# Expert weights reloaded half by half, an early buffer for expert 2's up weights, and more identity products

## The chip, the cores and the metric

The kernel runs on one core of a Trainium2 chip. The metric is the device time of one execution in microseconds (us). The kernel before took 1606.25 us, the median of three runs (1605.87 to 1609.35).

## What is computed

Two transformer blocks over 512 tokens of 1,024 features. The first has attention and a gated feed-forward part; the second has a state-space mixer, windowed attention and, last, a hierarchical mixture of experts. Only the end of the second block matters here:

```python
x = x + g1 * (jnp.concatenate([ssd_x, attn_x], axis=-1) @ w_out[layer])
h2 = rms_norm_2(x, norm2[layer]) * (1 + sc2) + sh2
moe_x = hier_moe(h2.reshape(b * n_tok, d), w_group[layer], b_group[layer], w_expert[layer],
                 b_expert[layer], w_gate[layer], w_up[layer], w_down[layer])
x = x + g2 * moe_x.reshape(b, n_tok, d)
...
return rms_norm_2(x, norm_final)
```

`hier_moe` picks for each token one of four groups and in it two of eight experts. There are 32 experts. Each has a gate and an up matrix of 1,024 x 512 and a down matrix of 512 x 1,024, all float32: 2.1 MB each (the trace writes 2048 KB), 6.3 MB an expert, 201 MB in all. Every matrix is used once.

## The kernel before

**Stages.** First block, second block's mixers, then `norm2_2`, then routing, then the expert stage. Routing computes the logits, the two best experts of each token, each token's place in its expert's block of 64 places, and a table from places to tokens. In the expert stage every expert works on one block of 64 places.

**Engines in routing.** PE makes the logits (ticks `halves` and `logits`), the ranks (`rank`), the table (`table`) and the rows of keys (`rows`). DVE computes what lies between in small steps (L2217 to L2309). Between `places` and `table` it computes the later blocks (L2298 to L2303), which PE doesn't wait for. While PE waits it multiplies the identity by itself (`unread`), with a result that nobody reads; each such product shows as two records.

**Expert n on the engines.** POOL gathers the 64 tokens of expert n from the stored normalised tokens in HBM by an indirect DMA (`gather`, L938), two experts ahead. PE transposes them (`tokens_in_place`, 8 transposes), DVE scales and shifts them (L2316, L2319), and PE multiplies them with gate and up (`gate_and_up`). That is one loop of KT = 8 steps over j; at j = 0 and j = 4 it waits for the first and the second half of both matrices, and the 32 records are two halves of the array's columns for gate and for up. ACT copies the result, PE transposes it (`hidden_transposed`), ACT and DVE form the hidden values (L2327), and PE multiplies with down (`down`, 16 records). PE also adds the results of a pair of experts to the tokens, two of four token tiles per expert (`pair_piece`, 32 records an odd expert has ahead of its gate products, 32 an even one has ahead of its down products, in two groups of 16). So the order on PE in a pair is: pieces, gate and up of the odd expert, transposes, a wait for DVE (L2327), its down; gate and up of the even expert, transposes, pieces, its down.

**Slots.** There are two sets of three slots of 2.1 MB: set 0 in the arena for even experts, set 1 in the ring for odd ones (`EXPERT_SLOTS`). One extra buffer, `early_gate`, lies over the normalised tokens once they have been stored to HBM (`h_stored`). It holds expert 2's gate, and no other weights.

**The order of the loads.** All weights are loaded by one queue, SP's, in this written order: expert 0 (six transfers, the halves of gate and up are 1 MB each and down is 2 MB); expert 1, once the output projection's last bank is filled; the store of the normalised tokens; expert 2's gate, in two halves, into `early_gate`, when the store has landed; expert 2's up and down into set 0; expert 3; the final gain; then a loop over experts 4 to 31. In `load_expert` (L757 to L779) SP waits for `gu_filled`, the count of experts whose gate and up products are done, and then issues all halves of gate and up; then it waits for `y_filled`, the count of finished down products, and issues down. Semaphores `first_in` and `second_in` count landed halves, `down_in` landed down matrices.

**Small state.** `sm` (`ssd_small`, 128 x 960 floats) is used by the state-space mixer and by the rows of the modulation, and no more from routing on. POOL's indirect and distance loads are written by a descriptor store in SBUF, of the size that the program asks for.

Of the kernel before, what the change touches and what calls it, by code (L numbers as in the profile page):

```python
# [14 lines left out]
P = 128  # L15
# [9 lines left out]
E = 32  # L25
# [133 lines left out]
def two_blocks(nc, consts_d, rope1_d, dist_d, h_d, inp, out):  # L159
    ctx = ExitStack()  # L160
    with ctx:
# [3 lines left out]
        def sb(name, shape, dt=F32):  # L165
            return ctx.enter_context(nc.sbuf_tensor(name, shape, dt))
# [28 lines left out]
        gains = sb("gains", [P, 6, KT])  # L195
        convw = sb("convw", [P, 224])
        ada_bias = sb("ada_bias", [P, 6, KT])
# [3 lines left out]
        mod_gain = sb("mod_gain", [P, 3, KT])  # L201
        gates = sb("gates", [P, 2, D])
        dt_bias, a_log = sb("dt_bias", [P, 16]), sb("a_log", [P, 16])
        d_skip, sinks, route_bias = sb("d_skip", [P, 8]), sb("sinks", [P, 8]), sb("route_bias", [P, 36])
# [6 lines left out]
        arena_at = nc.sbuf_base  # L211
        arena = sb("arena", [P, ARENA])


# [35 lines left out]
        def packed(size_of, start=0, of=arena, limit=ARENA):  # L250
# [6 lines left out]
            return views  # L257

        hT_flat = hT[:, :, :].rearrange("p j n -> p (j n)")
        ring_flat = ring[:, :, :].rearrange("p a n -> p (a n)")  # L260
# [33 lines left out]
        skip_x = carve(2048 + 2 * (T + CTX), 512, of=slot)  # L294
        sm = sb("ssd_small", [P, 10, 96])
        cat = xn
# [384 lines left out]
        index_ready, late_ready = sem("index_ready"), sem("later_block_ready")  # L681
        xt_filled, xt_scaled, xt_ready = sem("expert_x_filled"), sem("expert_x_scaled"), sem("expert_x_ready")
        gu_filled, gu_ready = sem("gate_up_filled"), sem("gate_up_ready")
        ht_filled, silu_ready, hid_ready = sem("hiddenT_filled"), sem("expert_silu"), sem("expert_hidden")
# [82 lines left out]

        def load_expert(sp, e, par, reuse, early=False):

            if reuse is not None:  # L770
                sp.wait_ge(gu_filled, reuse)
            for half in range(2):
                for i in range(2):
                    if i or not early:
                        load_rows(sp, e, par, i, half)
            if reuse is not None:
                sp.wait_ge(y_filled, reuse)
            sp.dma_start(EXPERT_SLOTS[3 * par + 2], inp["w_down_2"].rearrange("a e (p f) d -> (a e) p (f d)", f=4)[e]).then_inc(
                down_in[par], 16)  # L779

        def modulation(sp, parts):
# [22 lines left out]
        def _(sp):  # L804
# [34 lines left out]

            banks.filled(sp, ("out2", TT - 1, 1))  # L840
            load_expert(sp, 1, 1, None)
            normed.wait(sp, ("norm2_2", TT - 1, 0))
            sp.dma_start(h_d.rearrange("(t p) n -> p t n", p=P), xn[:, 0:TT, :]).then_inc(h_stored, 16)
# [3 lines left out]
            for half, landed in enumerate((first_in, second_in)):  # L847
                sp.wait_ge(landed[0], 16)
                load_rows(sp, 2, 0, 0, half, early_gate)
            load_expert(sp, 2, 0, 1, True)  # L850
            load_expert(sp, 3, 1, 2)
            sp.wait_ge(gu_filled, 3)
            sp.dma_start(final_gain, inp["norm_final_2"].partition_broadcast(P)).then_inc(final_in, 16)
            with sp.Fori(2, E // 2) as it:
                for par in range(2):
                    load_expert(sp, 2 * it + par, par, 2 * it + par - 1)
# [450 lines left out]
        def _(pe):  # L1307
# [379 lines left out]
            route_pe.tick(mm(ps[2][:, TT * E:2 * TT * E], C("one").broadcast_to([P, P]), hot, True, True), "rank")  # L1687
            unread(ps[3], 34)
            route.wait(pe, "places")
# [20 lines left out]

            def gate_and_up(n, par, kpar, gate=None):

                gate_w, up_w = EXPERT_SLOTS[3 * par] if gate is None else gate, EXPERT_SLOTS[3 * par + 1]
                pe.wait_ge(xt_ready, n + 1)
                for j in range(KT):
                    if j % 4 == 0:
                        for i in range(2):
                            pe.wait_ge((first_in, second_in)[j // 4][2 * par + i], 16 * kpar + 16)  # L1720
                    for half, w in enumerate((gate_w, up_w)):
                        last = mm(ps[1][half * BLK:(half + 1) * BLK, :], xT[:, par, j, :], w[:, j * EF:(j + 1) * EF],
                                  j == 0, j == KT - 1)
                last.then_inc(gu_filled, 1)

# [41 lines left out]

            unread(ps[0], 6)
            tokens_in_place(0, 0, 0)
            route_act.wait(pe, "rows")  # L1770
            for n in range(E):
                if n % 2 == 1:
                    for pair, t in pieces_of_turn(n):
                        pair_piece(pair, t)
                gate_and_up(n, n % 2, n // 2, early_gate if n == 2 else None)
                if n + 1 < E:
                    tokens_in_place(n + 1, (n + 1) % 2, (n + 1) // 2)
                hidden_transposed(n, n % 2)
                if n % 2 == 0:
                    for pair, t in pieces_of_turn(n):  # L1780
                        pair_piece(pair, t)
                down(n, n % 2, n // 2, n if n else None)
# [633 lines left out]
```

## Time and profile before

| | before |
|---|---|
| time, median of 3 runs | 1606.25 us |
| time of the profiled execution | 1606.26 us |
| span of the profiled execution | 1604.4 us |
| PE busy | 1499.6 us, 93% of the span |
| DVE busy | 913.7 us, 57% |
| ACT busy | 518.9 us, 32% |
| mean of the DMA engines' rate | 192 GB/s |
| mean granted TensorE clock | 0.98 of full |

The table is an average over stages with different limits. The page's slices are 40.1 us each, so slices 27 and 28 are routing and the start of the experts (1,043 to 1,123 us). A DMA row gives the time from issue to landing. A wait is put down to what ended it.

### The profile page before, as it was taken

Reading aid. Unit: us, or ns where it says so; the run is one execution under the profiler, and the core shown is the slowest. Engines: PE = TensorE matmul, PEld = TensorE weight load, DVE = VectorE, ACT = ScalarE, POOL = GpSimd, SP = SyncE. Lnnn points to the kernel's source line nnn. Section 1 sums busy time; section 2 is a strip of 40 time slices with the busy share of each in tenths; the row PEclk is TensorE's granted clock in tenths of the full one; section 3 lists DMA queues with packets and bytes.
Section 4 is the critical chain, followed back from the end, with each engine's and each line's share of the span. In section 5 each row is a group of like instructions: output and inputs, shape, how many; then the busy total and the mean of one; then the engine's idle time right before and its main releaser. Section 6 shows DMA issues by size and latency. Waiting matters only on the chain.

```text
span 1604.4 us, 21206 instructions
## 1 busy us (share of the span) xinstructions
PE 1499.6 (93%) x8171; PEld 1041.4 (65%) x8171; DVE 913.7 (57%) x1697; ACT 518.9 (32%) x938; POOL 99.3 (6%) x132
## 2 busy tenths in 40 slices
PE   7999998999999999999999897988999999999896
PEld 6776667888888878878887686873444444344343
DVE  4745774467787567753764677472444454344435
ACT  5445665333343332243426534221101101010112
POOL 0000000000000000000004132001101101000100
PEclk9999998999999999999999999999999999999998
DMA  8212011255544357613020000565999999999993
GB/s 254 78 54 73 2 50 50 70 173 140 155 130 120 110 171 271 212 39 119 27 69 11 1 1 3 208 262 206 414 399 405 410 401 411 399 405 402 410 411 160
DMA packets 112365, 308.39 MB, mean 192 GB/s; under 512 B 13983, under 2 KB 65535, under 8 KB 90763
## 3 DMA queue, kind: packets, MB, share of 16 engines
q1 hardware_dynamic: 108755, 299.08, 50.4%
q0 software_dynamic: 3200, 7.87, 1.6%
q8 instruction: 66, 1.08, 0.3%
q14 instruction: 32, 0.26, 0.0%
q10 hardware_dynamic: 312, 0.10, 0.0%
HBM read 306.99 MB, written 4.22 MB: 194 GB/s over the span
## 4 chain that ended last, share of the span: by engine, by line
PE 73%; DMA 9%; DVE 8%; ACT 4%; issue 3%; SPq 2%; POOL 0%; DVEq 0%; ACTq 0%; POOLq 0%
PE bank L1309 68%; DMA arena<-in_w_up 8%; PE bank L1312 5%; SPq L826 1%; DVE arena L2192 1%; DVE ring L2134 0%; DVE hTc L2316 0%; ACT weights_high L971 0%; SPq L766 0%; DMA ring<-in_w_in 0%; DVE x_res L2205 0%; DVE ring L2136 0%; DVE xn L2204 0%; DVE arena L2386 0%; ACT hT_high L1031 0%
## 5 line engine op out<-in xcount | busy, mean ns | idle before, releaser
L1309 PE MATMUL bank<-weights_high,hT_high 128*128 128x512 f32 (+2 forms) x736 | 255.1, 385 | 12.6 <-ACT arena L1058 5.3
L1807 DVE TENSOR_TENSOR weights_low<-ring,weights_high 128x2048 fp32r<-128x2048 f32 (+2 forms) x61 | 135.6, 2224 | 139.8 <-ACT weights_high L971 138.9
L1309 PE MATMUL bank<-weights_low,hT_high 128*128 128x512 f32 (+2 forms) x560 | 212.6, 380 | 0.0
L971 ACT ACTIVATE weights_high<-ring 128x2048 fp32r<-128x2048 f32 (+2 forms) x61 | 113.4, 1859 | 190.7 <-PE bank L1309 158.0
L1309 PEld LDWEIGHTS bank<-weights_high,hT_high 128*128 128x128 f32 x736 | 139.0, 189 | 40.3 <-issue 8.4
L1309 PE MATMUL bank<-hT_high,weights_high 128*128 128x512 f32 x416 | 163.8, 394 | 0.8 <-DVE hT_low L1845 0.8
L1309 PE MATMUL bank<-hT_high,weights_low 128*128 128x512 f32 x416 | 161.9, 389 | 0.0
L1309 PE MATMUL bank<-hT_low,weights_high 128*128 128x512 f32 x416 | 161.9, 389 | 0.0
L2316 DVE TENSOR_TENSOR hTc<-bank,mod_gain 128x512 f32<-128x512 f32 x32 | 22.1, 691 | 193.9 <-PE bank L1312 193.9
L1309 PE MATMUL bank<-arena,hTc 128*64 128x512 f32 x496 | 115.6, 601 | 7.3 <-DMA arena<-in_w_up 5.7
L1309 PE MATMUL bank<-ring,hTc 128*64 128x512 f32 (+1 forms) x544 | 121.4, 583 | 0.6 <-DMA ring<-in_w_up 0.6
L1309 PEld LDWEIGHTS bank<-weights_low,hT_high 128*128 128x128 f32 x560 | 106.1, 189 | 19.5 <-issue 0.2
L1309 PEld LDWEIGHTS bank<-hT_high,weights_high 128*128 128x128 f32 x416 | 78.1, 188 | 20.2 <-issue 3.4
L1276 ACT ACTIVATE hTc<-bank 128x512 f32<-128x512 f32 x32 | 19.1, 597 | 221.9 <-PE bank L1309 221.9
L1309 PE MATMUL bank<-ring,hT 128*64 128x512 f32 x256 | 71.8, 713 | 18.3 <-DVE hT L2327 18.3
L1309 PEld LDWEIGHTS bank<-hT_high,weights_low 128*128 128x128 f32 x416 | 78.1, 188 | 16.3
L1309 PEld LDWEIGHTS bank<-hT_low,weights_high 128*128 128x128 f32 x416 | 78.1, 188 | 16.0
L1309 PEld LDWEIGHTS bank<-ring,hTc 128*64 128x64 f32 (+1 forms) x544 | 41.6, 140 | 71.9 <-issue 70.8
L1309 PEld LDWEIGHTS bank<-arena,hTc 128*64 128x64 f32 x496 | 38.1, 138 | 76.9 <-issue 76.9
L1309 PE MATMUL bank<-weights_high,hT_low 128*128 128x512 f32 (+1 forms) x224 | 84.0, 375 | 0.0
L1288 ACT ACTIVATE expert_y_high<-arena 128x512 fp32r<-128x512 f32 x32 | 20.2, 631 | 192.9 <-DVE arena L2350 192.9
L1135 ACT ACTIVATE arena<-bank,convw 128x512 f32<-128x512 f32 x44 | 34.3, 778 | 145.8 <-PE bank L1309 145.8
(329 smaller groups left out, 2483.7 us busy)
## 6 DMA issues: line engine op xcount, KB each, us to landing
arena<-in_w_up SPq DMA_DIRECT2D x32, 1024.0 KB, 20.0
arena<-in_w_down SPq DMA_DIRECT2D x16, 2048.0 KB, 22.3
ring<-in_w_gate SPq DMA_DIRECT2D x32, 1024.0 KB, 17.6
ring<-in_w_up SPq DMA_DIRECT2D x32, 1024.0 KB, 19.6
ring<-in_w_down SPq DMA_DIRECT2D x16, 2048.0 KB, 21.9
arena<-in_w_gate SPq DMA_DIRECT2D x30, 1024.0 KB, 18.6
xn<-in_w_ada SPq DMA_DIRECT2D x48, 512.0 KB, 4.7
ring<-in_w_up SPq DMA_DIRECT2D x44, 512.0 KB, 5.2
```

What stands on the lines that cost most here:

```text
L826: sp.dma_start(dst, src).then_inc(more_in, 16)
L971: high_ready.tick(s.activation(part_view(w_high, key), raw_view(key), ACT.Copy), k)
L1135: tap_mid.tick(s.activation((conv_g, conv_v)[gv][:, f % 2, :], bank[:, :], ACT.Identity, scale=convw[:, 44 + ch:45 + ch], bias=convw[:, 13 ...
L1276: s.activation(gu[:, par, :], ps[1][:, :], ACT.Copy).then_inc(gu_ready, 1)
L1288: s.activation(y_high[:, place, :], y_scaled, ACT.Copy).then_inc(y_high_ready, 1)
L1309: return nc.tensor.matmul(o, lhsT, rhs, start=start, stop=stop)
L1312: return nc.tensor.transpose(o, i, ident[0:n, 0:n])
L1807: low_ready.tick(v.tensor_tensor(part_view(w_low, key), raw_view(key), part_view(w_high, key), ALU.subtract), k)
L2192: ins = v.tensor_scalar(decay[:, i % 3, g * 4 + h, :], bank[:, h * P:(h + 1) * P], sm[:, 7, a:a + 1], 0.0, ALU.subtract, ALU.min)
L2316: v.tensor_tensor(xT[:, par, :, :], ps[0][:, :].rearrange("p (j n) -> p j n", j=KT), wide(mod_gain[:, 2, :], BLK), ALU.mult).then_inc(xt_s ...
```

## The change

- A buffer `early_up` of one slot's size is added, and `sm` is laid over it. Expert 2's up weights are loaded into it in two halves, right behind expert 1's loads; expert 2's gate and up products read both early buffers. `convw` lies elsewhere, and the descriptor store shrinks (the new argument `dynamic_dma_scratch_size=4096`; the default is 16384).
- `load_expert` is split into `load_gate_and_up` and `load_down`. The first halves of a reload now wait for a new semaphore, `gu_half_done`, which PE increments after step j = 3 of the products, and the second halves for `gu_filled`.
- The order on SP's queue becomes: expert 2's gate; a wait for both matrices of expert 2; expert 4's gate and up; expert 2's down; expert 3; the final gain; expert 4's down; expert 5; then the loop from expert 6.
- The identity products go from 34 to 44 ahead of the table products, from 6 to 13 ahead of the first tokens' transposes, and 7 new ones lie between these and expert 0's products.

```diff
-        convw = sb("convw", [P, 224])
...
+        convw = sb("convw", [P, 224])
...
+        early_up = sb("early_up", [P, UNIT])
...
+        sm = carve(0, 10, 96, of=early_up)
...
-        sm = sb("ssd_small", [P, 10, 96])
...
+        gu_half_done = sem("gate_up_first_rows_done")
...
-        def load_expert(sp, e, par, reuse, early=False):
-
-            if reuse is not None:
-                sp.wait_ge(gu_filled, reuse)
-            for half in range(2):
-                for i in range(2):
-                    if i or not early:
-                        load_rows(sp, e, par, i, half)
+        def load_down(sp, e, par, reuse):
+
             if reuse is not None:
                 sp.wait_ge(y_filled, reuse)
...
+        def load_gate_and_up(sp, e, par, reuse):
+
+            for half, used in enumerate((gu_half_done, gu_filled)):
+                if reuse is not None:
+                    sp.wait_ge(used, reuse)
+                for i in range(2):
+                    load_rows(sp, e, par, i, half)
+
+        def load_expert(sp, e, par, reuse):
+
+            load_gate_and_up(sp, e, par, reuse)
+            load_down(sp, e, par, reuse)
...
             load_expert(sp, 1, 1, None)
+            for half, landed in enumerate((first_in, second_in)):
+                sp.wait_ge(landed[1], 16)
+                load_rows(sp, 2, 0, 1, half, early_up[:, :])
             normed.wait(sp, ("norm2_2", TT - 1, 0))
...
                 load_rows(sp, 2, 0, 0, half, early_gate)
-            load_expert(sp, 2, 0, 1, True)
+            for landed in first_in[0:2] + second_in[0:2]:
+                sp.wait_ge(landed, 32)
+            load_gate_and_up(sp, 4, 0, 1)
+            load_down(sp, 2, 0, 1)
             load_expert(sp, 3, 1, 2)
             sp.wait_ge(gu_filled, 3)
             sp.dma_start(final_gain, inp["norm_final_2"].partition_broadcast(P)).then_inc(final_in, 16)
-            with sp.Fori(2, E // 2) as it:
+            load_down(sp, 4, 0, 3)
+            load_expert(sp, 5, 1, 4)
+            with sp.Fori(3, E // 2) as it:
                 for par in range(2):
                     load_expert(sp, 2 * it + par, par, 2 * it + par - 1)
...
-            unread(ps[3], 34)
+            unread(ps[3], 44)
...
-                gate_w, up_w = EXPERT_SLOTS[3 * par] if gate is None else gate, EXPERT_SLOTS[3 * par + 1]
+                gate_w, up_w = EXPERT_SLOTS[3 * par:3 * par + 2] if early is None else early
...
+                    if j == 3:
+                        last.then_inc(gu_half_done, 1)
                 last.then_inc(gu_filled, 1)
...
-            unread(ps[0], 6)
+            unread(ps[0], 13)
             tokens_in_place(0, 0, 0)
+            unread(ps[1], 7)
             route_act.wait(pe, "rows")
...
-                gate_and_up(n, n % 2, n // 2, early_gate if n == 2 else None)
+                gate_and_up(n, n % 2, n // 2, (early_gate, early_up[:, :]) if n == 2 else None)
...
-    nc = bacc.Bacc("TRN2", target_bir_lowering=False, num_devices=1)
+    nc = bacc.Bacc("TRN2", target_bir_lowering=False, num_devices=1, dynamic_dma_scratch_size=4096)
```

## Rows read from the trace of the kernel before

**Rows 1.** The page's slices of 40 us: what the DMA engines moved.

```profile
GB/s 254 78 54 73 2 50 50 70 173 140 155 130 120 110 171 271 212 39 119 27 69 11 1 1 3 208 262 206 414 399 405 410 401 411 399 405 402 410 411 160
```

**Rows 2.** A window: busy time by engine, granted clock, DMA share, GB/s.

```profile
1330.00:1560.00 230.00, 215.56 (x1099) 92.07 (x1098) 96.08 (x157) 23.20 (x43) 17.94 (x27) 0.97 1.01 406
```

**Rows 3.** PE's waits, 1090 to 1600 us: total, times, longest.

```profile
PE bank L1309 <- DVE hT L2327: 19.6, 17, 1.2
PE bank L1309 <- DMA arena<-in_w_up: 5.7, 5, 2.4
...
PE bank L1309 <- DMA ring<-in_w_up: 0.6, 2, 0.3
```

**Rows 4.** The chain that ended last, expert stage: start, us, what.

```profile
1145.35 12.11 PE bank L1309 x48
...
1176.74 10.52 PE bank L1309 x48
...
1329.16 12.24 PE bank L1309 x48
...
1342.98 24.98 DMA arena<-in_w_up
...
1534.04 25.28 DMA arena<-in_w_up
```

**Rows 5.** SP's queue in order of time: start, time of the issue.

```profile
1053.42 0.38 SPq L843 DMA_DIRECT2D normed_tokens<-xn  x1
1071.21 0.80 SPq L766 DMA_DIRECT2D xn<-in_w_gate  x2
1099.24 0.80 SPq L766 DMA_DIRECT2D arena<-in_w_up  x2
...
1126.80 0.36 SPq L766 DMA_DIRECT2D arena<-in_w_gate  x1
```

**Rows 6.** The chain, first gather: start, us, what.

```profile
1083.98 3.69 DMA xn<-normed_tokens,token_index
```

**Rows 7.** DMA issues of two windows: KB each, median us to landing.

```profile
xn<-in_w_gate SPq DMA_DIRECT2D x2, 1024.0 KB, 6.5
...
arena<-in_w_up SPq DMA_DIRECT2D x2, 1024.0 KB, 22.2
xn<-normed_tokens,token_index POOLq DMA_INDIRECT x1, 8.9
```

**Rows 8.** Windows around expert 0, columns as in rows 2.

```profile
1080.00:1084.00 4.00, 4.00 (x23) 4.00 (x23) 1.39 (x6) 0.00 (x0) 0.20 (x2) 0.57 0.00 0
...
1092.00:1096.00 4.00, 4.00 (x16) 1.56 (x14) 0.00 (x0) 0.00 (x0) 0.00 (x0) 0.75 0.06 18
...
1096.00:1100.00 4.00, 4.00 (x24) 1.89 (x20) 0.00 (x0) 0.60 (x1) 0.00 (x0) 1.00 0.00 0
1100.00:1116.00 16.00, 13.61 (x69) 5.73 (x69) 6.50 (x12) 1.99 (x4) 2.86 (x4) 1.00 0.86 313
1100.00:1148.00 48.00, 44.45 (x227) 18.86 (x227) 20.65 (x34) 5.21 (x10) 5.65 (x8) 0.97 0.96 378
```

**Rows 9.** PE in order of time: start, us, operation, [idle before].

```profile
1068.96 7.76 PE L1309 MATMUL bank<-const 128*128 128x128 f32 x68
1079.27 2.81 PE L1309 MATMUL bank<-arena 128*128 128x94 f32 x16 [2.55 <-DVE arena L2296]
...
1087.81 1.06 PE L1312 MATMUL bank<-const,xn 64*128 64x64 f32 x8 [1.73 <-DMA xn<-normed_tokens,token_index]
1090.43 8.78 PE L1309 MATMUL bank<-arena,hTc 128*64 128x512 f32 x32 [1.55 <-issue]
...
1105.63 7.04 PE L1309 MATMUL bank<-ring,hTc 128*64 128x512 f32 x32
```

**Rows 10.** DVE in order of time, end of routing.

```profile
1080.77 0.16 DVE L2303 CAST later_blocks<-later_counts 1x15 int32<-1x15 f32 x1
1082.19 0.21 DVE L2307 TENSOR_SCALAR arena<-bank 128x47 f32<-128x47 f32 x1 [1.26 <-PE bank L1309]
```

More of the change, by code:

```diff
@@ L1709, in tokens_in_place, with gate_and_up @@
                 last.then_inc(xt_filled, 1)
-            def gate_and_up(n, par, kpar, gate=None):
-                gate_w, up_w = EXPERT_SLOTS[3 * par] if gate is None else gate, EXPERT_SLOTS[3 * par + 1]
+            def gate_and_up(n, par, kpar, early=None):
+                gate_w, up_w = EXPERT_SLOTS[3 * par:3 * par + 2] if early is None else early
                 pe.wait_ge(xt_ready, n + 1)
```

## The prediction, made before the changed kernel was run

> **What bounds the kernel now.** I read the page's slices first. From the 29th slice on (1,123 us) the rate stands at 399 to 414 GB/s until the last slice but one; the three slices ahead of it, in which the first experts' weights come in and routing runs, have 206 to 262 [rows 1]: the expert stage streams weights as fast as they come, and there is room ahead of it. A window over the second half of that stage has the DMA engines at a share of 1.01 with 406 GB/s, while PE is busy 215.56 of 230 us [rows 2]. Both are nearly full, so the next view is PE's waits. From expert 0's first product to the end of the stage PE waits for weights 5.7 + 0.6 = 6.3 us, and 17 times for about 1.2 us on DVE's addition to the tokens (L2327), which the change leaves [rows 3]. The chain says where the 6.3 us lie: up to 1,329 us it holds only PE's own pace, and from 1,343 us on it goes through the landing of an up half [rows 4].
>
> Two rates follow. PE's pace: the products after the gap recur at 1145.35 and, six pairs of experts later, at 1329.16: 183.81 / 6 = 30.64 us a pair. The weights' pace: expert 18's second up half lands at 1342.98 + 24.98 = 1367.96, expert 30's at 1534.04 + 25.28 = 1559.32, six pairs too: 191.36 / 6 = 31.89 us a pair [rows 4]. So DMA is 1.25 us a pair slower than PE. It begins with a lead, uses it up at about expert 18, and then PE waits. What a change in the loads is worth is decided by the lead, and it is worth at most the 6.3 us that PE waits; anything more has to come from PE's own path.
>
> **Part 1, expert 2's up weights into a buffer of their own.** Two transfers of 1 MB each are issued right behind expert 1's, ahead of the store of the normalised tokens at 1053.42 [rows 5]. Their own waits on SP are for expert 0's halves, which were issued some 37 us earlier; they cost nothing. The queue is full there: SP's next issue, which waits for the store to land, comes 17.8 us after the store's, at 1071.21 [rows 5]; the landing is at about 1070.8. 2.1 MB at 406 GB/s [rows 2] are 5.2 us, so the store lands at about 1076.0, and SP's next two issues (expert 2's gate) move to about 1076.4. Behind SP's wait stand only the later weights. Behind the store stands also the first gather, issued at 1083.98 [rows 6]: 8 us of cover, 6.8 after the gain of part 3, so it costs nothing. The gate transfers take 6.5 us to landing [rows 7] and land at about 1083.6 instead of 1078.4; the first gather's own data follow its issue, then at 1082.8, by more than a microsecond. They just miss each other (rival 2).
>
> **Part 2, reloading by halves, and expert 4's gate and up ahead of expert 2's down.** Before, the queue is empty from about 1078 to 1100 (0 GB/s in 1096 to 1100) [rows 8], since the up slot is reloaded only at 1099.24, the slot of expert 0's gate lies unused until 1126.80, and from 1100 to 1116 the share is only 0.86 [rows 5, 8]. After, expert 4's first halves go out when four of expert 0's eight steps are done, its second halves after the other four. With expert 0 starting at 1089.2 and lasting 7.04 us (part 3) these are 1092.8 and 1096.3, 4.2 MB; expert 2's down (2.1 MB) goes out at about 1102.7, expert 3's halves at 1106.0 and 1109.5 (2.1 MB each): from 1094 to 1116 there is always something queued. Bytes by 1116: before, 16 us at 313 GB/s, 5.0 MB [rows 8]; after, 22 us x 0.406 = 8.9 MB, and 2.1 MB of part 1 lie in place: 6.0 MB or 15 us more. This lead isn't all kept. With expert 3's weights in, the slots are full, and PE sets when they come free; by about 1148 all that the slots allow is loaded, which I sum to 22.8 MB (18.9 of weights from expert 4's gate to expert 5's up, 0.5 of final gain, 1.3 of gathers, 2.1 early) against 48 us x 378 GB/s = 18.1 MB before [rows 8], a lead of 4.7 MB or 11.5 us; a restart of an empty queue takes about 1 us (issue at 1099.24, data from about 1100) [rows 5, 8]. Say 10 us. From there DMA falls back by 1.25 us a pair, as before, with no more empty stretches. PE comes to the same place 3.0 us earlier (part 3), so the weights are ahead of their old place by 10 - 3.0 = 7 us as PE sees them. The deficit was 6.3 us. So all waits for weights should go, with 0.7 us to spare at expert 30: **-6.3 us**, and the bound is then PE alone. What is late next is that pace of 30.64 us a pair, with the 1.2 us gap on L2327. The added semaphore increment on an instruction that is there anyway shows in no row; the nearest ones, the increments on each last product, leave no visible gap, so its cost is 0, at most some tenths over 32 experts. SP's new waits (gu_half_done) have only weights behind them; expert 5's loads stand behind the wait for expert 3's down, as before.
>
> **Part 3, more identity products.** In two windows of 4 us the granted clock is 0.57 at 1080 to 1084 and 0.75 at 1092 to 1096, where full is 1.00 [rows 8]: the lower of the two levels, 1.2 instead of 2.4 GHz, for part of each. What PE did before: it was idle 2.55 us ahead of 1079.27, and 1.73 and 1.55 us ahead of 1087.81 and 1090.43 [rows 9]. Ten more products are 20 records at 7.76 / 68 = 0.114 us, 2.3 us: the row ends at 1076.72 + 2.3 = 1079.0, just inside 1079.27. Seven more (1.6 us) go ahead of the first gather's arrival, seven new ones (1.6 us) between its transposes and expert 0's products (gap 1.55). All three fit their gaps by some tenths, and if each overran by that, it would cost 0.3 us in all.
> - The table products: 16 records of 94 columns take 2.81 us [rows 9]. At full clock an estimate from the 0.114 us for 128 columns is 16 x 0.084 + 0.15 = 1.5 us, 1.3 less. But DVE is busy with the later blocks until 1080.77 + 0.17 = 1080.94, and reads the table from 1082.19 now [rows 10]: it can't start before 1081.0, so the gain is 1.2 us, not 1.3. The token index, POOL's gather (3.69 us, [rows 6]) and expert 0 follow at the same distance: **-1.2 us**.
> - Expert 0's 32 products take 8.78 us, expert 1's 7.04 [rows 9]: **-1.7 us** if the clock holds.
> Bounds: 0 if the clock falls anyway, -3.0 if both hold; I take both, since the long gaps go and the one that is left, about 1.0 us ahead of the gather, is no longer than gaps of 1.2 us that at full clock PE mostly passes.
>
> **Part 4, addresses and the smaller descriptor store.** Moved small tiles cost nothing that a row shows. Fewer descriptors could make POOL's gathers wait for older ones; no row shows such a wait. A gather is issued one expert (15 us) ahead of its use and lands in 8.9 us in the full queue [rows 7]; bounds 0 and 0.5 us, I take 0.
>
> **The sum** against the profiled execution: span 1604.4, its time 1606.26 (1.9 around it), equal to the median of 1606.25. 1606.25 - 1.2 - 1.7 - 6.3 = **1597.0 us**. Bounds of the terms: 0 to 1.2, 0 to 1.7, and 3 to 6.3.
>
> **The rivals.**
> 1. *DMA stays the bound.* The lead is 0.7 us too large in my sum, and 10 us is made of a 11.5 and a guess of the losses. If halves give more empty moments while PE sets the pace, or the rate is 402 rather than 406 GB/s (1%, 4 us over the stage), 2 to 4 us of waiting remain at experts 26 to 30. For: shares of 1.01 all along [rows 2]. Against: the lead's size. Time 1599 to 1601.
> 2. *The start gains nothing.* The gate transfers and the first gather overlap. In an empty queue a gather takes 3.69 us of the chain [rows 6]; in the full one the issue-to-landing time is 8.9 us [rows 7], against about 4.7 counted the same way: up to 4 us more on the critical path, which cancels part 3. Then expert 0 starts late, the weights are further ahead, and only the 6.3 us go: 1600 to 1601. For: a margin of 1 us. Against: the gate's last bytes, not its landing, are what counts.
> The Trainium skill (DMA: Bandwidth & Descriptors, section Queues, rings and completion order) says that each DMA engine takes turns between the queues that have work, a packet at a time, so that a gather isn't held until the weights ahead of it are done. By that rule an overlap costs less than the rest of the gate transfers, and the start would keep part of its 3 us, which makes about 1598; the gathers of the full queue agree, since they land in 8.9 us where an up half issued beside them takes 22.2 [rows 7].
> 3. *The clock falls at every gap* (slower). Every second pair has a cold stretch: 48 products take 12.11 us at 1145.35 and 10.52 at 1176.74 [rows 4], 1.6 us. There are 17 gaps of 1.2 us [rows 3] and seven such cold stretches before the last expert. If an earlier start shifts things so that each gap is followed by one, ten more cost 16 us, and the 1.7 of expert 0 is lost too: 1606.25 - 9.2 + 17.7 = 1614.8. It decides from six more on; eight make it slower by over 0.2%. Against: a cold stretch delays the next gap, and the pattern of every second pair held over 250 us.
> The Trainium skill (TensorE: Matmul & The Clock Gate, section Part 1: The HAM clock gate) says that the watch on activity runs freely and isn't tied to the kernel. By it one cold stretch more or less is chance, 1.6 us either way, and no run of before here can show which.
> 4. *Fewer cold stretches*, or a lead that also hides a gap: 1592 to 1595.
>
> **Chances.** Forecast (1595 to 1599) 0.55; rival 1 0.16; rival 2 0.12; rival 3 0.05; rival 4 0.07; the change brings less than 3.2 us by several of these together 0.05. Two runs of one kernel differ here by about 0.2%, 3.2 us, and less than that can't be told from no change. Faster by more: 0.55 + 0.16 + 0.12 + 0.07 = 0.90, less 0.02 for the ends of rivals 1 and 2; same 0.07; slower 0.05. The range reaches over rivals 1 and 2 and part of 4: 1593.5 to 1601.5, leaving out about 0.17.
>
> **What would show it.** Right: no wait of PE for in_w_up, or under 1 us; DMA at over 300 GB/s from 1094 and below that once around 1126 to 1135 and again near 1148; expert 0's products at 1089.2 in 7.04 us; clock 1.00 from 1076 to 1096; pairs still at 30.6 us. Wrong: waits for weights from expert 24 on (rival 1), a first gather over 4.5 us (rival 2), 12.1 us for the 48 products in each pair (rival 3), the store landing after 1081.

## The result

The changed kernel takes 1597.87 us, the median of 13 runs (1594.51 to 1604.32), beside 1606.66 us of the kernel before in 13 runs (1604.28 to 1610.44). The ratio is 0.9947, with a 95% interval of 0.9937 to 0.9956: 8.5 us faster, 7.1 to 10.1. The forecast was 1597.0 us and 9.2 us faster.

The page of the changed kernel: the span, PE's busy time, and the rate in slices of 39.8 us.

```profile
span 1593.5 us, 21287 instructions
...
PE 1497.4 (94%) x8219; PEld 1043.0 (65%) x8219; DVE 914.3 (57%) x1697; ACT 519.2 (33%) x938; POOL 99.4 (6%) x132
...
GB/s 255 71 62 74 1 48 54 53 178 152 133 145 115 98 180 269 240 27 133 27 54 27 1 1 1 211 263 274 354 404 412 409 409 407 399 407 393 410 412 178
```

The profiled execution took 1595.31 us, in the faster half of the 13 runs. Against [rows 1] the 28th slice rises from 206 to 274 GB/s, since bytes come earlier, and the 29th falls from 414 to 354, since there is a dry moment in it. The rate afterwards is the same.

PE's waits from 1085 to 1600 us: total, times, longest. They answer to [rows 3].

```profile
PE bank L1326 <- DVE hT L2347: 19.6, 17, 1.2
PE bank L1326 <- DMA arena<-in_w_up: 1.9, 2, 1.4
PE bank L1329 <- DMA xn<-normed_tokens,token_index: 1.0, 1, 1.0
```

The 5.7 + 0.6 us of waiting for weights have become 1.9 us; the 17 gaps on DVE stand as they were. They are on the step that forms the hidden values (L2327 before, L2347 after), which the prediction called the addition to the tokens.

The chain that ended last in the changed kernel: start, us, what. It answers to [rows 4] and [rows 6].

```profile
1083.57 3.63 DMA xn<-normed_tokens,token_index
...
1143.32 10.52 PE bank L1326 x48
...
1327.18 10.52 PE bank L1326 x48
...
1492.49 27.06 DMA arena<-in_w_up
...
1523.93 26.15 DMA arena<-in_w_up
```

Six pairs take 1327.18 - 1143.32 = 183.86 us, 30.64 a pair, as before. A landing enters the chain only from 1492 us on, where before it did from 1343 on.

PE around the start of the experts: start, us, operation, and in brackets the idle time before. It answers to [rows 9].

```profile
1069.32 9.99 PE L1326 MATMUL bank<-const 128*128 128x128 f32 x88
1079.64 2.02 PE L1326 MATMUL bank<-arena 128*128 128x94 f32 x16 [0.33 <-DVE arena L2316]
1081.50 1.98 PE L1326 MATMUL bank<-const,arena 128*128 128x128 f32 x16
...
1087.34 1.06 PE L1329 MATMUL bank<-const,xn 64*128 64x64 f32 x8 [0.96 <-DMA xn<-normed_tokens,token_index]
1088.33 1.83 PE L1326 MATMUL bank<-const 128*128 128x128 f32 x14
1090.09 7.09 PE L1326 MATMUL bank<-arena,hTc 128*64 128x512 f32 x32
```

The gaps of 2.55, 1.73 and 1.55 us are 0.33, 0.96 and none. The table products take 2.02 us instead of 2.81 and expert 0's products 7.09 instead of 8.78.

Windows of the changed kernel, columns as in rows 2; they answer to [rows 8].

```profile
1100.00:1148.00 48.00, 45.56 (x234) 19.02 (x236) 19.76 (x33) 5.04 (x10) 4.74 (x7) 1.00 0.93 366
1148.00:1330.00 182.00, 175.03 (x906) 75.59 (x904) 80.20 (x131) 19.15 (x36) 16.71 (x24) 0.97 1.01 408
1128.00:1132.00 4.00, 4.00 (x22) 1.47 (x20) 3.11 (x6) 0.00 (x0) 0.00 (x0) 1.00 0.13 44
...
1080.00:1084.00 4.00, 4.00 (x38) 4.00 (x38) 1.72 (x8) 0.48 (x1) 0.61 (x2) 1.00 0.97 408
```

The clock at 1080 to 1084 is full where it was 0.57. The queue now runs dry once, at 1128 to 1132, where all slots are full and PE sets the pace. Its issues in order of time show the new order; they answer to [rows 5].

```profile
1053.76 0.38 SPq L855 DMA_DIRECT2D normed_tokens<-xn  x1
1077.29 0.81 SPq L768 DMA_DIRECT2D xn<-in_w_gate  x2
1093.86 0.33 SPq L768 DMA_DIRECT2D arena<-in_w_gate  x1
...
1097.22 0.33 SPq L768 DMA_DIRECT2D arena<-in_w_gate  x1
```

**Where the time went.** The issue of expert 1's first load lies at 1046.98 us before and at 1047.32 after, so I count from there to the end of the span: 557.4 us before, 546.2 after, 11.2 less. On PE's side:

- To expert 0's first product: 43.45 and 42.77 us, 0.7 less. Expert 0's products: 1.7 less.
- Waits for weights: 4.4 less. Each such wait costs about 0.17 us beyond the idle time shown: 16 products without a wait take 3.44 us from start to start, those ahead of a wait take that, the idle time and 0.17. Five waits fewer are 0.8 us.
- Cold stretches (the granted clock is at the lower level, and a set of 16 products takes 1.65 us longer): the trace's clock record has eight between 1100 us and the last products before (from 1145, 1207, 1268, 1329, 1391, 1456, 1521 and 1582 on) and six after (from 1203, 1265, 1295, 1357, 1418 and 1480 on), 3.3 less.

These are 10.9 of the 11.2 us. The queue's side gives a shorter account. In both executions PE still waits for expert 30's second up half. Its products start again, when that half has landed, 512.5 us after expert 1's first load before and 502.9 after: 9.6 us earlier. What follows takes 1.7 us less, since before it held the cold stretch of 1582 and after it holds none. So in both the landing of these weights sets the end, and what PE gained on its way there, at the start and by one cold stretch fewer, counts only as far as the queue came earlier too.

The gain of this pair of executions is larger than the 8.5 us of all runs; two cold stretches less may be no more than chance.

### The profile page after: what moved, and what is told of

Its sections match the earlier page's. It is cut to its first block, busy times and chain, and to the rows that moved or that the text cites. A ratio compares the mean times of both kernels' runs of the same rounds, so it can differ in the third digit from the quotient of the medians.

```text
span 1593.5 us, 21287 instructions
## 1 busy us (share of the span) xinstructions
PE 1497.4 (94%) x8219; PEld 1043.0 (65%) x8219; DVE 914.3 (57%) x1697; ACT 519.2 (33%) x938; POOL 99.4 (6%) x132
## 4 chain that ended last, share of the span: by engine, by line
PE 78%; DVE 9%; ACT 4%; DMA 4%; issue 3%; SPq 1%; POOL 0%; DVEq 0%; ACTq 0%; POOLq 0%
PE bank L1326 72%; PE bank L1329 6%; DMA arena<-in_w_up 3%; SPq L835 1%; DVE arena L2212 1%; DVE hTc L2336 1%; DVE ring L2154 0%; ACT weights_high L988 0%; DMA ring<-in_w_in 0%; DVE hT L2347 0%; DVE x_res L2225 0%; DVE ring L2156 0%; DVE xn L2224 0%; DVE arena L2406 0%; ACT hT_high L1048 0%
## 5 line engine op out<-in xcount | busy, mean ns | idle before, releaser
L1326 PE MATMUL bank<-arena,hTc 128*64 128x512 f32 x480 | 106.1, 593 | 1.9 <-DMA arena<-in_w_up 1.9
L1326 PE MATMUL bank<-ring,hT 128*64 128x512 f32 x256 | 68.6, 685 | 18.4 <-DVE hT L2347 18.4
L2356 DVE TENSOR_TENSOR x_res<-bank,x_res 128x512 f32<-128x512 f32 x128 | 79.4, 683 | 2.3 <-PE bank L1326 1.3
```

The lines of the kernel that those rows point to most:

```text
L1326: return nc.tensor.matmul(o, lhsT, rhs, start=start, stop=stop)
L2356: last = v.tensor_tensor(side, ps[4 + 2 * (t % 2) + half][:, :], side, ALU.add)
```

## The experiments

Each kernel ran in turn with the kernel before on the same chip. "Stage" is the time from expert 1's first load to the end of the span, as above, in the profiled execution. "Last landing" is the time from the same load to where expert 30's products go on after their wait for the second up half; it tells how far ahead the queue is. Us, from the traces:

| kernel | last landing | stage | cold stretches after expert 0's first products |
|---|---|---|---|
| before | 512.5 | 557.4 | 8 |
| changed | 502.9 | 546.2 | 6 |
| 1, identity products only | 510.1 | 553.4 | 5 |
| 1, all but these | 509.4 | 552.7 | 8 |
| 2, halves only | 510.4 | 553.6 | 6 |
| 2, changed without halves | no wait there | 552.6 | 9 |
| 4, gaps filled | 502.6 | 546.0 | 0 |
| 5, gate beside the gather | 510.4 | 553.7 | 6 |

**1. The parts apart.** First only the identity products, in the kernel before:

```diff
-            unread(ps[3], 34)
+            unread(ps[3], 44)
...
-            unread(ps[0], 6)
+            unread(ps[0], 13)
             tokens_in_place(0, 0, 0)
+            unread(ps[1], 7)
```

> The kernel before with only the added identity products (44, 13 and 7). Theory (the start and the weights are separate terms): expert 0 starts 0.7 us earlier and its products take 7.0 us instead of 8.8. In the kernel before the reloads hang on PE's progress, so the queue starts 2.4 us earlier too, and the whole stage moves: 1606.7 - 2.4 = 1604.3 us. Rival (the weights are the bound and the start is hidden behind them): no change, 1606.7, with PE waiting 8.7 us for in_w_up instead of 6.3.

Measured: ratio 0.9984 (0.9970 to 0.9999), 2.6 us faster. PE's waits in this kernel:

```profile
PE bank L1309 <- DMA arena<-in_w_up: 9.0, 7, 2.2
...
PE bank L1309 <- DMA ring<-in_w_up: 0.6, 1, 0.6
```

The theory holds: the last landing comes 2.4 us earlier (512.5 to 510.1), just what PE's start gives, since the reloads hang on PE and come earlier too. The waits rise all the same, from 6.3 to 9.6 us: this execution has two cold stretches fewer ahead of expert 30 than that of the kernel before (five against seven), and the 3.3 us that PE gained there it spent waiting for weights.

Then everything but the identity products:

```diff
-            unread(ps[3], 44)
+            unread(ps[3], 34)
...
-            unread(ps[0], 13)
+            unread(ps[0], 6)
             tokens_in_place(0, 0, 0)
-            unread(ps[1], 7)
```

> The changed kernel with the identity products of before (34, 6 and none). Theory: the waits of PE for in_w_up fall from 6.3 us to under 1.9, since PE comes 2.4 us later and the weights don't; expert 0's products take 8.8 us. 1597.9 + 2.4 - 1.5 = about 1599 us, at most 1600.3. Rival (the identity products carry the gain): 1604 or more.

Measured: ratio 0.9958 (0.9944 to 0.9972), 6.7 us faster. PE's waits:

```profile
PE bank L1329 <- DMA xn<-normed_tokens,token_index: 2.2, 1, 2.2
...
PE bank L1326 <- DMA arena<-in_w_up: 1.2, 1, 1.2
```

The waits fall to 1.2 us and the time to about where it was expected. Over all runs the loads carry most of the gain, the start 2 to 3 us: 2.6 + 6.7 = 9.3 us beside 8.5 for both together. In this trace they don't add up so simply. The last landing is 3.1 us earlier than before, where the two parts together give 9.6: expert 0's products take 10.02 us here and its down products are cold too, and as long as SP waits for PE to free the slots, each such loss delays the loads behind it.

**2. The halves.** Only the halves, in the kernel before:

```diff
-            if reuse is not None:
-                sp.wait_ge(gu_filled, reuse)
-            for half in range(2):
+            for half, used in enumerate((gu_half_done, gu_filled)):
+                if reuse is not None:
+                    sp.wait_ge(used, reuse)
                 for i in range(2):
```

> The kernel before with nothing but the first halves of gate and up reloaded once step 3 is done. Theory (the lead in bytes ahead of the PE-bound stretch decides): only the up half of expert 2 goes out 4 us earlier, 1 MB, and expert 3's first halves; the empty moments before 1116 us shrink. The lead grows by 2 to 4 us, PE's waits fall to 2 to 4 us: 1603 to 1605 us. Rival (finer reloading raises the rate while DMA is the bound): the rate over 1330 to 1560 us rises above 406 GB/s and the waits vanish: 1600.

Measured: ratio 0.9982 (0.9971 to 0.9993), 2.9 us faster, which is within what was expected. The profiled execution has 6.5 us of waits for weights, no fewer than the 6.3 before, but it has one cold stretch fewer ahead of expert 30 (six against seven), 1.7 us by which PE came earlier. The lead did grow: the last landing comes 2.1 us earlier (512.5 to 510.4), at the low end of the 2 to 4 expected, and the first wait for weights comes at expert 22 instead of 18. The rate over 1330 to 1550 us is 405 GB/s, so finer reloading doesn't raise the rate, and that rival falls.

Then the changed kernel without them:

```diff
-            for half, used in enumerate((gu_half_done, gu_filled)):
+            for half, used in enumerate((gu_filled, gu_filled)):
```

> The changed kernel with both halves waiting for the whole of the products, all else kept. Theory (lead): the first 2.1 MB of expert 4 go out 3.5 us later, at 1097.2 instead of 1093.9, and the queue has an empty moment at each expert while PE sets the pace, so the lead is 3 to 4 us smaller and PE's waits rise from 1.9 to 5 or 6 us: 1601 us. Rival (early buffer alone carries the lead): 1598, no difference from the changed kernel.

Measured: ratio 0.9969 (0.9957 to 0.9981), 5.0 us faster than before, 3.5 us of the changed kernel's gain lost; the two intervals just miss each other. The first 100 us from expert 1's first load, in the kernel before, the changed one and this one, and PE's waits in this one:

```profile
1046.98:1146.98 100.00, 85.30 (x508) 51.32 (x508) 49.68 (x143) 16.14 (x34) 11.20 (x15) 0.96 0.74 287
```

```profile
1047.32:1147.32 100.00, 89.85 (x572) 55.12 (x572) 50.02 (x144) 16.15 (x34) 11.21 (x15) 1.00 0.83 323
```

```profile
1046.94:1146.94 100.00, 89.59 (x558) 54.82 (x559) 49.72 (x143) 16.16 (x34) 11.23 (x15) 0.97 0.77 301
```

```profile
PE bank L1326 <- DMA arena<-in_w_up: 2.9, 2, 2.4
```

301 instead of 323 GB/s over 100 us are 2.2 MB or 5.4 us of lead lost, more than the 3 to 4 expected; of the 3.6 MB that the changed kernel is ahead of the kernel before, 1.4 are left. Part of it isn't the halves' own: expert 0's down products are cold in this execution (from 1101 us on), so PE frees the slots 1.7 us later; by that estimate some 3.7 us are the halves'. The waits rise by 1.0 us only, because PE too is slower here, by three cold stretches more than in the changed kernel. So the halves are worth 2.9 us of time in the kernel before and 3.5 in the changed one. This execution ends without a wait at expert 30, by PE's pace, so how their lead becomes these 3.5 us it doesn't show.

**3. The lead, measured by itself.** With most of the token pieces' products left out PE is soon ahead of the weights, and the queue's own schedule sets the end. The same edit went into the kernel before and into the changed one:

```diff
-                for k, place in enumerate(places):
-                    for part, y in enumerate((y_high, y_low)):
+                for k, place in enumerate(places[-1:]):
+                    for part, y in enumerate((y_high,)):
```

> The kernel before with two of the eight products of each token piece, so that PE does 3 us less in each pair of experts (three quarters of the sums are left out). PE is then faster than the weights from the start, and the end of the stage shows where the queue's own schedule ends. Theory: weights bound throughout, pairs at 31.9 us; PE, which waited 6.3 us at the end, waits far more, and the time stays near 1604 to 1606 us, less the last 1 us of pieces.

> The same products left out in the changed kernel. Theory (lead of 10 us): the changed queue's own schedule ends 9 to 11 us ahead of that of the kernel before, so the two light kernels differ by that, and this one ends at about 1595 us, no more than 2 us ahead of the changed kernel itself, whose margin was nearly used up. Rival (the changed kernel is PE-bound with room to spare): it ends 5 us or more ahead of the changed kernel, at 1592 or less.

Measured: ratios 0.9973 (0.9961 to 0.9984) and 0.9916 (0.9901 to 0.9931), medians 1602.23 and 1594.00 us; the first a little under the 1603 to 1605 expected. The two differ by 0.0057, 9.2 us; their stages, 552.4 and 543.3 us, by 9.1. PE waits for weights 21 and 20 times, from 1194 and from 1248 us on; first the light kernel before, then the light changed one:

```profile
PE bank L1309 <- DMA arena<-in_w_up: 21.9, 12, 3.0
PE bank L1309 <- DMA ring<-in_w_up: 13.5, 9, 2.7
```

```profile
PE bank L1326 <- DMA ring<-in_w_up: 13.9, 10, 2.6
PE bank L1326 <- DMA arena<-in_w_up: 13.5, 10, 2.6
```

So the lead is 9.2 us (forecast: 10). How near the changed kernel comes to its queue's own end is less sure. By the profiled executions the light changed kernel's stage is 2.9 us shorter, of which about 0.9 are pieces left out behind the last expert (from DVE's last step on expert 31's result to the start of DVE's last step on the output it takes 9.75 us instead of 10.64), so 2 us are left. By the ratios of all runs (0.9916 against 0.9947) it is 5.0 us faster, 4 without these pieces: more than the 2 expected and near the rival's 5. The profiled execution of the changed kernel is one of its faster ones; in the slower ones PE may have more of its own to lose, which no trace here shows.

**4. The clock's gaps filled.** In the changed kernel, five identity products in each gap of 1.2 us:

```diff
-                pe.wait_ge(hid_ready, n + 1)
-                pe.wait_ge(down_in[par], 16 * kpar + 16)
                 if read is not None:
                     pe.wait_ge(y_weighted, read)
+                if isinstance(n, int) and (n % 2 == 1 or n == 0):
+                    unread(ps[3], 5)
+                pe.wait_ge(hid_ready, n + 1)
+                pe.wait_ge(down_in[par], 16 * kpar + 16)
```

> The changed kernel with five identity products in each of the 1.2 us gaps ahead of an odd expert's down products (and expert 0's), into the bank that these products overwrite. Theory (weights and PE end together): the cold stretches between 1100 and 1550 us, six in the changed kernel, become fewer or vanish, PE's pair goes to 29.8 us, and PE then waits for weights instead: waits rise from 1.9 to about 10 us, and the time falls by 1 us at most, 1597 to 1598. Rival (PE alone is the bound): 1588 to 1590, 1.6 us for each cold stretch that goes. Second rival: the fill overruns the gap in each pair and costs 0.1 to 0.3 us each, 2 to 4 us slower.

Measured: 1595.76 us, ratio 0.9927 (0.9914 to 0.9941). Between 1100 us and the last products no cold stretch is left. A set of 48 products in the chain, as each pair has it, and PE's waits:

```profile
1330.14 10.54 PE bank L1326 x48
```

```profile
PE bank L1326 <- DMA arena<-in_w_up: 10.0, 7, 2.4
...
PE bank L1326 <- DMA ring<-in_w_up: 0.4, 1, 0.4
```

The pair goes to 29.8 us, and the waits rise from 1.9 to 10.4 us: in these two executions what the clock gives, the queue takes. The last landing is 502.6 us, the changed kernel's 502.9, and the stage 546.0 against 546.2. Over all runs it is faster than the changed kernel by 2.1 us by the medians and 3.2 by the ratios, more than the 1 us expected; the intervals overlap, so whether it beats it isn't settled.

The same with the queue out of the way. From expert 6 on only half of each down matrix is loaded (the products use stale rows for the other half), without and with filled gaps:

```diff
+            n = UNIT if isinstance(e, int) else HALF
+            sp.dma_start(EXPERT_SLOTS[3 * par + 2][:, 0:n],
+                         inp["w_down_2"].rearrange("a e (p f) d -> (a e) p (f d)", f=4)[e][:, 0:n]).then_inc(
```

> The changed kernel with only half of each down matrix loaded from expert 6 on (the products use stale rows for the other half), a sixth less bytes, so the queue can't be the bound. Theory (the changed kernel is PE-bound but for 1.9 us): PE's waits for weights are 0, pairs at 30.65 us, and the time is 1.5 to 2.5 us under the changed kernel, 1595.5 to 1596.5. Rival (the weights' traffic itself slows PE, ACT or DVE): pairs under 30.3 us and 1590 or less.

> The same with the 1.2 us gaps filled as in e7. Theory (in the changed kernel PE's clock and the queue each hide the other's gain): no cold stretch, no wait, pairs at 29.8 us, 10 us under e9: 1585 to 1587. Rival (filling a gap costs what the clock gives): within 3 us of e9.

Measured: 1597.1 us, ratio 0.9938 (0.9922 to 0.9954), and 1584.11 us, ratio 0.9854 (0.9837 to 0.9870). Neither waits for weights. The chain of the first, then of the second:

```profile
1144.43 12.19 PE bank L1328 x48
...
1328.34 12.22 PE bank L1328 x48
```

```profile
1145.71 10.52 PE bank L1328 x48
...
1324.55 10.52 PE bank L1328 x48
```

183.91 us for six pairs against 178.84: 30.65 and 29.81 us a pair. A sixth less bytes alone give 1.4 us by the ratio, and nothing that can be told from the changed kernel; the pairs keep their 30.65 us, so traffic doesn't slow PE. Filling the gaps on top of that gives 13.5 us more (0.0084, and 13.5 by the stages). It is the cold stretches: the first has nine from 1100 us on, 14.9 us at 1.65 each, and the second none, but one earlier, in the fill ahead of expert 0's products (14 records in 3.10 us instead of 1.83), 1.6 us with what it adds to these products. So PE and queue end together in the changed kernel: fewer bytes alone give 1.4 us, filled gaps alone 2 to 3, both together 15.

**5. The rival of the first gather.** Expert 2's gate load is held back until the table products are done:

```diff
             route_pe.wait(sp, "halves")
+            route_pe.wait(sp, "table")
             sp.wait_ge(h_stored, 16)
```

> The changed kernel with expert 2's gate load held back until the table products are done, so that its 2.1 MB run beside the first gather. Theory (price of the overlap that the prediction named as a rival): the first gather takes 2 to 4 us longer than 3.6, expert 0 starts that much later, and expert 4's halves follow. The later start is partly made good by fewer waits: 1599.5 to 1601.5 us. Rival, by the rule of the Trainium skill that the engines take turns between queues (DMA: Bandwidth & Descriptors, section Queues, rings and completion order): under 1.5 us longer, 1598 to 1599.5.

Measured: 1603.48 us, ratio 0.9976 (0.9965 to 0.9987), 4.7 us of the gain lost by the ratio. The gather in the chain, and two microseconds in which PE is idle while the DMA engines are full:

```profile
1084.19 7.97 DMA xn<-normed_tokens,token_index
```

```profile
1088.00:1090.00 2.00, 0.00 (x0) 0.00 (x0) 0.00 (x0) 0.00 (x0) 0.00 (x0) 1.00 1.05 324
```

The packets of SP's queue (q1, the weights) and POOL's (q0, the gathers), first in 1085 to 1088.3 us, then in 1088 to 1091: count, MB, share.

```profile
q1 hardware_dynamic: 188, 1.41, 101.4%
```

```profile
q0 software_dynamic: 140, 0.36, 53.1%
q1 hardware_dynamic: 63, 0.39, 37.9%
```

The gather takes 7.97 instead of 3.63 us, 4.3 more, not far from the 5.2 us of the 2.1 MB it ran beside. It was issued at 1084.19 us; up to 1088.3 only weights move, then both share the engines. PE, idle for 5.29 us, then has a cold stretch, and expert 0's products take 7.84 us. Expert 0's products end 6.6 us later than in the changed kernel, and the last landing comes 7.5 later: the start's delay goes into the queue in full. Both of my sizes for the whole were too small: 1599.5 to 1601.5 and less were expected.

**6. The small descriptor store alone,** in the kernel before:

```diff
-    nc = bacc.Bacc("TRN2", target_bir_lowering=False, num_devices=1)
+    nc = bacc.Bacc("TRN2", target_bir_lowering=False, num_devices=1, dynamic_dma_scratch_size=4096)
```

> The kernel before with nothing but the descriptor store at 4096 bytes. Theory: no gather or distance load waits for a descriptor, 1606.7, within 1 us of the kernel before; gathers still land 8 to 9 us after issue. Rival: gathers land later, and PE waits for tokens: 1608 or more.

Measured: ratio 1.0001 (0.9988 to 1.0014). Gathers land 8.3 us after their issue, against 8.1 in a like stretch of the kernel before; both stages are 557.4 us, both last landings 512.5. No cost shows.

**7. More lead.** Experiment 4 with both early buffers used a second time, for expert 5, and expert 7's gate and up loaded into the ring one turn earlier:

```diff
+            for half, used in enumerate((gu_half_done, gu_filled)):
+                sp.wait_ge(used, 3)
+                for i, into in enumerate((early_gate, early_up[:, :])):
+                    load_rows(sp, 5, 1, i, half, into)
             load_down(sp, 4, 0, 3)
...
+            load_gate_and_up(sp, 7, 1, 4)
+            load_down(sp, 5, 1, 4)
+            load_expert(sp, 6, 0, 5)
...
-                gate_and_up(n, n % 2, n // 2, (early_gate, early_up[:, :]) if n == 2 else None)
+                gate_and_up(n, n % 2, n // 2, (early_gate, early_up[:, :]) if n in (2, 5) else None)
```

> e7 with both early buffers used once more, for expert 5's gate and up, issued at about 1121 to 1124 us instead of 1137 to 1140, and expert 7's then in the ring at 1137 to 1140 instead of 1167 to 1170. Theory (the lead in bytes decides, and it grows by what the queue stood empty): the empty stretch at 1128 to 1132 goes, the lead grows by 2 to 4 us, PE's waits for weights fall from 10.4 to 6 to 8 us, and the time from 1595.8 to 1592 to 1594. Rival (order in the queue matters more: expert 7's early bytes delay expert 6's): no gain or a loss, 1596 to 1598.

Measured: 1595.08 us, ratio 0.9926 (0.9911 to 0.9940), no different from 0.9927. Windows of it:

```profile
1100.00:1148.00 48.00, 47.79 (x264) 22.88 (x264) 20.66 (x34) 5.82 (x11) 5.65 (x8) 1.00 1.01 412
1148.00:1330.00 182.00, 181.72 (x988) 82.81 (x986) 81.71 (x133) 19.60 (x37) 16.72 (x24) 1.00 1.00 399
1176.00:1180.00 4.00, 3.95 (x20) 1.35 (x20) 1.39 (x4) 0.00 (x0) 0.67 (x1) 1.00 0.55 195
```

The dry moment at 1128 is gone: 412 instead of 366 GB/s, 2.2 MB more by 1148 us. Then the queue runs dry at 1176, since expert 7's weights are in and the slots are full again: 399 instead of 408 GB/s over 182 us, 1.6 MB less. 0.6 MB or 1.5 us of lead remain, not the 2 to 4 us expected (the last landing is 501.0 us, 1.6 earlier than in experiment 4), and they don't show in the time. The waits fall to 7.8 us, and one cold stretch came back, behind a wait of 2.5 us. My theory was too simple: a buffer used once shifts the dry moment by a turn; it must stay in the rotation, for the down weights too, to keep its bytes. That wasn't tried.

## Why the prediction was right

**The waits for weights** were the largest term. The step "all waits should go, with 0.7 us to spare" failed by its size: 1.9 us stay, at experts 28 and 30, and 4.4 of 6.3 us went, inside the bounds of 3 to 6.3. The lead of "say 10 us" is 9.2 us by experiment 3, and 9.6 by the last landings of the two executions. PE came to expert 30 2.4 us earlier by the start and 1.7 earlier by one cold stretch fewer on the way (six against seven), which the sum hadn't: 9.2 - 2.4 - 1.7 = 5.1 us against a deficit of 6.3, so 1.2 should stay, and 1.9 did. "The bound is then PE alone" is thus not what this trace shows: the landing at expert 30 still decides, by 0.5 us. The dry moment at 1126 to 1135 came as forecast; the second, near 1148, did not. Expert 4's halves went out at 1093.86 and 1097.22, some 1 us later than summed, half of it because the start gave less.

**The start** was mis-sized. Forecast 1.2 us, measured 0.7. The failed step is the estimate of 1.5 us for the table products at full clock, which scaled a record's time by its columns. They take 2.02 us, and 16 records of 128 columns right behind them take 1.98: 94 columns save nothing here. So DVE reads them 0.8 us earlier, not 1.2. The rest is in the last fill: seven identity products take 1.83 us with their tail, not 1.6, and expert 0's products start when these end, not on the tokens. **Expert 0's products** gave 1.7 us, as forecast.

**Nothing paid for the early buffer**, as forecast: the store landed 5.7 us later (5.2 forecast), still 6 us ahead of its use, and the first gather took 3.63 us. The gate's landing and the gather just miss each other, and experiment 5 shows what was at stake. Rival 2 had named up to 4 us, with 4.7 us for the gather in an empty queue as counted from its issue. That was misread: the trace gives 3.7 us for it either way, so its rows allowed 5.2 us more; measured are 4.3. The Trainium skill's rule (DMA: Bandwidth & Descriptors, section Queues, rings and completion order) that the engines take turns between queues led me to a lower price beside it. Experiment 5 bears it out only in part: from 1088.35 us on both queues move data side by side, but for the first 4.2 us after the gather's issue only weights moved, where in the changed kernel its data begin 1.7 us after the issue. The measured price decides.

**The clock.** Rival 3 didn't come: cold stretches follow at most every second gap, with one exception in this execution (at 1265 and 1295, two pairs in a row). They are less regular than [rows 4] suggests, and their number may be part of what makes this profiled execution 2.6 us better than the median. The Trainium skill (TensorE: Matmul & The Clock Gate, section Part 1: The HAM clock gate) says that the watch on activity runs freely. No run here tests that; six, eight and nine cold stretches in kernels with the same gaps fit it.

**Right for the right reason?** In the main: experiments 1 to 3 show both sources, the queue's lead and the start, and experiment 4 shows that both bounds meet at the end. But the closeness of 1597.0 to 1597.87 is partly luck. The three terms as measured make 0.7 + 1.7 + 4.4 = 6.8 us, not 9.2, and all runs have 8.5. In the profiled pair waits that no longer occur (0.8) and fewer cold stretches (3.3), which the sum had at nothing, more than made good the difference; for the other runs no trace shows what did. Nor were the two terms as separate as the sum had them, since the queue's lead hangs on PE's start.

## What to carry to other kernels

Where two engines have nearly the same pace, sum the lead of the slower one at its start and what it loses per turn; the gain of an edit to the slower one's lead is at most what the faster one waits. As long as the loads wait for PE to free their slots, a microsecond lost by PE at the start is a microsecond lost by the queue at the end (experiments 1 and 5). Filling bytes into a quiet stretch ahead pays until PE becomes the bound; here filled gaps gave 2 to 3 us with all the bytes to load and 13.5 with a sixth fewer. Keep the one small transfer on the critical path clear of large ones, by order of issue and not by hope.

To compare two profiled executions, count from a mark in the stage and not from the start of the span, and look for the last wait that both share.

## What the runs showed that I had not expected

A gather of 64 rows issued 1.8 us behind 2.1 MB of weights on another queue takes 7.97 us, 3.63 in an empty one. Yet in the always full queue gathers land 8.1 us after their issue, where the weights issued beside them take 13 to 19: there they do get past part of what is queued. What the 8 us consist of isn't shown.

Gaps of 1.2 us each, which follow PE's transposes, are enough to bring the lower clock again and again. Five identity products in each took all cold stretches out of the two kernels of experiment 4 (29.81 against 30.65 us a pair), at no cost to the gap: a pair without a cold stretch takes 29.8 us unfilled too (from 1176.74 to 1206.55 us in the kernel before). Whether the transposes have a part in it wasn't tried.

Executions of one kernel differ by up to 10 us (1594.5 to 1604.3 in the changed one), and part of it arises ahead of the experts. The profiled execution of experiment 6 has the same stage of 557.4 us as the kernel before, but gets there 8.3 us later. The kernel before, then that of experiment 6, from 980 to 1000 us:

```profile
980.00:1000.00 20.00, 16.74 (x138) 15.29 (x139) 10.77 (x26) 11.29 (x27) 5.01 (x4) 0.91 0.00 1
```

```profile
980.00:1000.00 20.00, 15.99 (x109) 14.15 (x107) 9.43 (x22) 8.56 (x23) 5.88 (x5) 0.74 0.00 1
```

The mixers' end has a granted clock of 0.74 instead of 0.91 there. Whether the cold stretches cause all of the 8.3 us wasn't tried.
